# Gate projections of the first block: two matmuls a step instead of three, halves added on VectorE

## The chip, the cores and the metric

The kernel runs on one core of one Trainium2 chip. The metric is the device time of one execution, in microseconds (us). The engines are TensorE (PE, with its weight loads as PEld), VectorE (DVE), ScalarE (ACT), GpSimd (POOL) and SyncE (SP), which issues the weight DMAs.

## The reference, cut to what matters

The program is two transformer blocks on 256 tokens of width 1024, in float32. The first one is hybrid attention: a windowed grouped-query attention (16 heads, "swa") and a differential attention (8 heads, "diff"), each followed by a branch projection, and merged with sigmoid gates. The gates are what is changed here.

```python
proj = u @ w_in[l]                      # u: rms-normed tokens, w_in: 1024 x 6656
qa, ka, va, qb, kb, vb, g = jnp.split(proj, SPLITS, axis=-1)   # g: the last 2048 columns
...
gates = jax.nn.sigmoid(g + b_gate[l])
g_swa, g_diff = gates[..., :D_MODEL], gates[..., D_MODEL:]
merged = g_swa * (o_swa @ w_branch_swa[l]) + g_diff * (o_diff @ w_branch_diff[l])
```

After it come an output projection, a feed-forward block, and the whole second block (delta rule, sparse attention, cross-attention, feed-forward), which the change does not touch.

## The kernel before, in words

**Products.** Float32 products are made of three products of the shorter type fp32r. Each weight unit of 1024 x 256 (or as many elements in another shape) is loaded into `raw`. ScalarE rounds it to `whi` (high part), VectorE subtracts to get `wlo` (low part), both in two halves of 128 output features: `split(i, k)`. The activations `R1` are kept as high and low parts too, for 256 tokens side by side in one buffer (`R1b`). `feat` (lines 823 to 825) makes a half of a unit: for each of 8 slices of the contraction, high weights by high rows, high weights by low rows, low weights by high rows, each a matmul of 256 columns, all into the same 256 columns of a PSUM bank. That is 24 matmuls with 24 weight loads.

`wide` (lines 847, 848) is the form that the feed-forward blocks use: high weights by high and low rows in one matmul of 512 columns, into the two halves of a PSUM bank, then low weights by high rows into the first half. That is 16 matmuls. VectorE adds the two halves of the bank (`summed`, line 1617, a TENSOR_REDUCE).

**Gates.** There are 8 gate units of 256 features (u = 0 to 7), each of two halves j of 128. `gate` on TensorE goes through `pair`, which claims one of the three banks of the pool "gemm" for both halves and calls `feat`. On ScalarE `gate` waits for the second half and then makes two activations, tanh(0.5 x + 0.5 b), from the bank into `GA`. Later VectorE multiplies the branch projections by (1 + `GA`), in `bsw` and `bdf`.

**Order.** `schedule` writes one list of steps, by hand, and each engine goes through this list and does its own part of each step, in that order. Between the engines there are semaphores only. The units of weights stand in the order ka0, va, qa1, gate 0, qa2, gate 1, qa3, gate 2, qb0, vb0, kb0, gate 3, qb1, vb1, kb1, gate 4, qb2, vb2, kb2, gate 5, qb3, vb3, kb3, gate 6, four branch units, gate 7. The heads are woven in between: each head has stages at fixed distances (`STAGES`, `STARTS`), such as scores (L968), maxima (`s0`, `s1`: L1370 or L1519 on VectorE), exponentials (ScalarE), scaling (`n`: L1367), transposes of the probabilities (`p0`, `p1`: L809), copies of these (PT 0 by ScalarE, PT 1 by VectorE at L1504, the part for the meta tokens at L1506 or L1538), the product with V (L998 and L1003, or L1041 and L1044 for diff heads) and the output. Splits are put into the list some two units ahead of the half that uses them; a split waits until the half that used the same buffer is done.

So for the step of a gate half each engine's queue holds, around the second half of gate unit 0, for example: `split(6,0)`, scaling of head 0, gate half 1, scores and first maxima of head 1, `split(6,1)`, second maxima, exponentials, a rope unit of qa, and the two probability copies of head 0.

ScalarE's helper for activations is line 1986, VectorE's helpers are lines 1364 (scalar_tensor_tensor), 1367 (tensor_scalar) and 1370 (tensor_tensor_reduce); transposes are line 809 and the low split is line 1374. In the rows a tile name tells more than the line: `whi` is the high split, `SE<-ps,st` the tanh of a gate, `SC`, `SD` or `SE<-ps 32x256` a rope copy, `SC<-ps 128x512` the copy of PT 0.

**Banks.** The eight PSUM banks are split into "gemm" (three) and "head" (five). `claim` takes the bank whose last reader stands earliest in the list, and makes TensorE wait for that reader.

Of the kernel before, what the change touches and what calls it, by code (L numbers as in the profile page):

```python
# [10 lines left out]
ACT = mybir.ActivationFunctionType  # L11
AX = mybir.AxisListType.X
MUL, ADD, SUB, MAX = ALU.mult, ALU.add, ALU.subtract, ALU.max
# [495 lines left out]
def program(nc, A, out):  # L509
    with ExitStack() as ctx:  # L510
# [12 lines left out]
        R1 = (R1b[:, 0], R1b[:, 1], R1b)  # L523
# [16 lines left out]
        def signal(name, by=1):  # L540
            signals.append(Signal(ctx.enter_context(nc.semaphore(name)), now, by))
            return signals[-1]
# [7 lines left out]
        hi_split, lo_split = signal("hi_split"), signal("lo_split")  # L550
        gemm = signal("gemm")
# [1 line left out]
        norm_pe, norm_act, norm_dve, norm_pool = [signal("norm_" + n) for n in ("pe", "act", "dve", "pool")]  # L553
        rope_act, rope_dve, rope_pool = [signal("rope_" + n) for n in ("act", "dve", "pool")]
        val_pe, val_act, val_dve = [signal("val_" + n) for n in ("pe", "act", "dve")]
        swap_act, gate_act = signal("swap_act"), signal("gate_act")
        head_pe, head_act, head_dve, head_pool = [signal("head_" + n) for n in ("pe", "act", "dve", "pool")]
        merge_act, merge_dve, merge_pool = [signal("merge_" + n) for n in ("act", "dve", "pool")]
        post_act, post_dve, post_pool = [signal("post_" + n) for n in ("act", "dve", "pool")]
# [16 lines left out]
        def ps(*key):  # L576
            return held[key]
# [4 lines left out]
        def stat(key, n):  # L582
            if key not in stats:
                stats[key] = st[:, room[0]:room[0] + n]
                room[0] += n
                assert room[0] <= 512
            return stats[key]

        ident = ca[:, 0:128]
        half = stat("half", 16)  # L590

        def caf(name):
            return ca[:, CA[name][0]:CA[name][0] + CA[name][1]]
# [55 lines left out]
        GA = SE[:, 0:4096].rearrange("p (b n) -> p b n", b=16)  # L649
# [44 lines left out]
        rsb = {s: caf("band")[:, 256 * i:256 * i + 256] for i, s in enumerate(("nf1", "nf2"))}  # L694
# [12 lines left out]
        def normed(s):  # L707
            return lambda kt, t=1: (norm_dve, (s, "lo", kt))
# [86 lines left out]
        def tensor(e, counting):  # L795
            p = Lane(e, counting)

            def claim(pool, key, *freed):

                b = next_bank(pools[pool])  # L800
                for signal_, k in b.freed:
                    p.wait_ge(signal_, k)
                b.freed = freed
                held[key] = b.t
                return b.t
# [10 lines left out]
            def feat(o, i, j, R, n, ready, *keys):  # L816

                hi, lo = unit(i)
                c = slice(j * 128, j * 128 + 128)
                p.wait_ge(lo_split, (i, j))  # L820
                for kt in range(8):
                    p.wait_ge(*ready(kt))
                    e.matmul(o, hi[:, kt, c], R[0][:, kt, 0:n], start=kt == 0, stop=False)  # L823
                    e.matmul(o, hi[:, kt, c], R[1][:, kt, 0:n], start=False, stop=False)  # L824
                    m = e.matmul(o, lo[:, kt, c], R[0][:, kt, 0:n], start=False, stop=kt == 7)  # L825
                m.then_inc(gemm(("half", i, j), ("unit", i), *keys))

            def featk(B, i, part, R, ready, key):

                hi, lo = unit(i)  # L830
                p.wait_ge(lo_split, (i, part))
                for kt in range(4 * part, 4 * part + 4):
                    p.wait_ge(*ready(kt))
                    for j in range(2):
                        o, c = B[:, 256 * j:256 * j + 256], slice(j * 128, j * 128 + 128)
                        e.matmul(o, hi[:, kt, c], R[0][:, kt, 0:256], start=(kt, j) == (0, 0), stop=False)  # L836
                        e.matmul(o, hi[:, kt, c], R[1][:, kt, 0:256], start=False, stop=False)  # L837
                        m = e.matmul(o, lo[:, kt, c], R[0][:, kt, 0:256], start=False, stop=(kt, j) == (7, 1))  # L838
                m.then_inc(gemm(("half", i, part), ("unit", i), key))
# [210 lines left out]
            def pair(kind, u, j, i, pool, R, ready, *freed):  # L1050
                if j == 0:
                    claim(pool, (kind, u), *freed)
                if order[i][1] == "featk":
                    return featk(ps(kind, u), i, j, R, ready, (kind, u))
                feat(ps(kind, u)[:, 256 * j:256 * j + 256], i, j, R, 256, ready, (kind, u))

            def gate(u, j, i):
                pair("gate", u, j, i, "gemm", R1, normed("n1"), (gate_act, u))

            def bsw(u, j, i):  # L1060
                pair("bsw", u, j, i, "gemm", R3a, lambda kt: (head_dve, ("ol", nth["swa", kt])), (merge_dve, ("bs", u)))
# [262 lines left out]
            def cross(h, part):  # L1324
# [17 lines left out]
                if part == "o":  # L1342
                    B = claim("four", ("xo", h), (cross_dve, ("ox", h)))
                    p.wait_ge(cross_dve, ("pt", h))
                    for j in range(2):
# [3 lines left out]
                    m.then_inc(cross_pe(("xo", h)))  # L1349

            parts = {"turn": turn, "turnx": turnx, "rsb": rsb_, "rope": rope, "ropek": ropek, "turnm": turnm, "v": v, "vt": vt, "swa": swa, "diff": diff, "gate": gate, "bsw": bsw, "bdf": bdf,
                     "out": out_, "mem": mem, "upg": upg, "upu": upu, "down": down, "tail": tail, "conv": conv, "zg": zg,
                     "delta": delta, "dsa": dsa, "dsah": dsah, "xq": xq, "cross": cross}
# [6 lines left out]
        def vector(e, counting):  # L1360
            d = Lane(e, counting)
# [237 lines left out]
            def chunk(u):  # L1599
# [8 lines left out]
                for t in range(2):  # L1608
                    d.wait_ge(post_dve, ("p1", t, u))
                    e.tensor_tensor(X[:, t, c], X[:, t, c], junk["p1"][:, 1024 + 1024 * t:2048 + 1024 * t][:, c], ADD).then_inc(post_dve(("p1", "x", u, t)))  # L1610

            def summed(kind, f, j, b):

                B = ps(kind, f, j, b)
                at = 256 * b + (512 if kind == "u" else 0)
                d.wait_ge(gemm, (kind, f, j, b))
                e.tensor_reduce(FSLOT[j % 2][0][:, at:at + 256], B[:, :].rearrange("p (a n) -> p n a", a=2), AX, ADD).then_inc(  # L1617
                    ffn_dve((kind, f, j, b)))
# [12 lines left out]
            def upg(f, j, part, i):  # L1631
                if j in WIDE:
                    summed("g", f, j, part)
                if part and j:
                    scaled_gate(f, j)
# [297 lines left out]
            def final():  # L1933
# [33 lines left out]
                for hf in range(2):  # L1967
# [4 lines left out]

            e.memset(half, -0.5).then_inc(set_dve("half"))
            e.memset(ones, 1.0).then_inc(set_dve("one"))
            parts = {"split": split, "rows": rows, "turn": turn, "turnx": turnx, "stat": stat_, "rsb": rsb_, "chunk": chunk, "chunk2": chunk2, "upg": upg, "setup": setup, "rotate": rotate, "turnm": turnm, "vt": vt, "swa": swa, "diff": diff,
                     "bsw": bsw, "bdf": bdf, "post": post, "upu": upu, "zc": zc, "tail": tail, "taps": taps, "zg": zg,
                     "delta": delta, "dsa": dsa, "dsah": dsah, "add": add, "squares": squares, "cross": cross, "final": final}
            for now[0], (name, *a) in enumerate(plan):
# [3 lines left out]
        def scalar(e, counting):  # L1982
            a = Lane(e, counting)

            def act(o, i, f=ACT.Copy, **kw):
                return e.activation(o, i, f, **kw)  # L1986
# [124 lines left out]
            def gate(u, j, i):  # L2111
                if j:
                    a.wait_ge(pc_in, 0)
                    a.wait_ge(gemm, ("gate", u))
                    a.wait_ge(set_dve, "hb")
                    for k in range(2):
                        act(GA[:, 2 * u + k, :], ps("gate", u)[:, 256 * k:256 * k + 256], ACT.Tanh,
                            bias=hb[:, 2 * u + k:2 * u + k + 1], scale=0.5).then_inc(gate_act(u))

            def merge(u):  # L2120
# [227 lines left out]
            def final():  # L2348
# [6 lines left out]
                for hf in range(2):  # L2355
# [10 lines left out]
            e.dma_start(pc[:, 0:8], A["params"][:, 0:8]).then_inc(mix_in(0), 16)  # L2366
            parts = {"split": split, "rows": rows, "turn": turn, "turnx": turnx, "stat": stat_, "setup": setup, "rope": rope, "roped": roped, "turnm": turnm, "swap": swap, "v": v, "swa": swa,
                     "diff": diff, "gate": gate, "merge": merge, "mem": mem, "psq": psq, "post": post, "upg": upg, "upu": upu, "conv": conv,
                     "convs": convs, "zg": zg, "delta": delta, "dsa": dsa, "dsah": dsah, "squares": squares, "xq": xq, "cross": cross,
                     "final": final}  # L2370
# [189 lines left out]
        for _ in range(2):  # L2560
            for engine in (tensor, vector, scalar, gpsimd, sync):
                engine(Count(), True)
            rewind()
# [6 lines left out]
        @block.vector  # L2570
        def _(e):
            vector(e, False)
# [57 lines left out]
```

## Time and profile before

| | us |
|---|---|
| median of 3 runs | 960.5 (960.37 to 960.55) |
| the profiled execution | 960.5 |
| its span | 958.4 |
| TensorE busy | 937.5 (98%), 6180 matmuls |
| VectorE busy | 674.6 (70%) |
| ScalarE busy | 527.3 (55%) |
| GpSimd busy | 137.9 (14%) |

The span runs from the first to the last instruction; what is over in the execution's time lies around it. Matmuls are pipelined, and the ends of their rows are modelled, so their rows overlap: what a matmul costs is read from where the next one starts. The granted clock of TensorE is 0.999 over the span, that is 2.4 GHz throughout. A line of the timeline has the start (us from the span's start), the duration, the engine, line, operation, tiles, shapes, how many instructions are merged in it, and in brackets the idle time of the engine before it with what ended it.

### The profile page before, as it was taken

The numbers are of one execution on the slowest core, as the hardware profiler recorded it, in microseconds if no ns is written. First come the engines' busy times: TensorE is split into PE (matmuls) and PEld (weight loads), VectorE is DVE, ScalarE is ACT, GpSimd is POOL, SyncE is SP. The second block draws the span as 40 slices with busy tenths as digits, with TensorE's granted clock in tenths as the row PEclk, the third lists the DMA queues.
The fourth block names the chain that finished last, engine by engine and source line by source line (L and its number), as shares of the span: only waits on it lengthen the run. The fifth ranks groups of instructions, "written<-read, shape, count | busy, mean of one in ns | idle before, by whom it ended". The sixth has DMA issues, their size and how long they took to land.

```text
span 958.4 us, 15483 instructions
## 1 busy us (share of the span) xinstructions
PE 937.5 (98%) x6180; PEld 840.1 (88%) x6180; DVE 674.6 (70%) x1233; ACT 527.3 (55%) x1013; POOL 137.9 (14%) x159
## 2 busy tenths in 40 slices
PE   8999999999999999999999999899999999999996
PEld 7989888999999988888898899888798898888885
DVE  6888777777478676776758668767665567666765
ACT  6876665875456644444446686455454454344443
POOL 2211111220133000000001119941100000000001
PEclk9999999999999999999999999999999999999999
DMA  9544324343367555555565563300543455656441
GB/s 316 183 155 132 128 93 136 129 133 133 133 229 243 169 204 194 176 194 198 176 216 185 177 237 123 121 30 1 176 149 117 153 176 176 220 176 205 166 156 45
DMA packets 115863, 154.71 MB, mean 161 GB/s; under 512 B 2728, under 2 KB 98224, under 8 KB 115536
## 3 DMA queue, kind: packets, MB, share of 16 engines
q1 hardware_dynamic: 113376, 142.91, 44.9%
q0 software_dynamic: 1952, 10.42, 3.0%
q8 instruction: 49, 0.80, 0.4%
q10 hardware_dynamic: 464, 0.40, 0.2%
q14 instruction: 22, 0.18, 0.1%
HBM read 150.56 MB, written 3.16 MB: 160 GB/s over the span
## 4 chain that ended last, share of the span: by engine, by line
PE 89%; DVE 3%; POOL 3%; ACT 3%; issue 1%; DMA 0%; POOLq 0%; DVEq 0%; ACTq 0%
PE ps L847 14%; PE ps L823 8%; PE ps L825 8%; PE ps L824 8%; PE ps L848 7%; PE ps L1135 4%; PE ps L1108 4%; PE ps L1109 4%; PE ps L1110 4%; PE ps L866 4%; PE ps L868 4%; PE ps L867 4%; PE ps L809 3%; PE ps L836 2%; PE ps L838 2%; PE ps L837 2%
## 5 line engine op out<-in xcount | busy, mean ns | idle before, releaser
L1374 DVE TENSOR_TENSOR wlo<-raw,whi 128x1024 fp32r<-128x1024 f32 (+1 forms) x268 | 327.7, 1242 | 164.4 <-ACT whi L1986 164.0
L1986 ACT ACTIVATE whi<-raw 128x1024 fp32r<-128x1024 f32 (+1 forms) x268 | 273.8, 1050 | 129.9 <-PE ps L848 53.5
L847 PE MATMUL ps<-R1b,whi 128*128 128x512 f32 x576 | 201.8, 393 | 0.0
L823 PE MATMUL ps<-R1b,whi 128*128 128x256 f32 (+1 forms) x592 | 172.3, 291 | 0.8 <-DVE wlo L1374 0.8
L825 PE MATMUL ps<-R1b,wlo 128*128 128x256 f32 (+1 forms) x592 | 167.7, 283 | 0.0
L824 PE MATMUL ps<-R1b,whi 128*128 128x256 f32 (+1 forms) x592 | 167.5, 283 | 0.0
L848 PE MATMUL ps<-R1b,wlo 128*128 128x256 f32 x576 | 161.4, 280 | 0.0
L847 PEld LDWEIGHTS ps<-R1b,whi 128*128 128x128 f32 x576 | 108.1, 188 | 24.7 <-issue 0.5
L823 PEld LDWEIGHTS ps<-R1b,whi 128*128 128x128 f32 x592 | 111.6, 188 | 9.1 <-issue 7.9
L825 PEld LDWEIGHTS ps<-R1b,wlo 128*128 128x128 f32 x592 | 111.8, 189 | 0.0
L824 PEld LDWEIGHTS ps<-R1b,whi 128*128 128x128 f32 x592 | 111.5, 188 | 0.2
L848 PEld LDWEIGHTS ps<-R1b,wlo 128*128 128x128 f32 x576 | 108.2, 188 | 0.6
L2380 POOL TENSOR_TENSOR st<-st 128x1 f32<-128x1 f32 (+5 forms) x28 | 23.3, 838 | 375.4 <-DVE st L1367 299.8
L1108 PE MATMUL ps<-whi,R3ah 128*128 128x512 f32 x176 | 68.8, 391 | 0.0
L1109 PE MATMUL ps<-wlo,R3ah 128*128 128x512 f32 x176 | 68.8, 391 | 0.0
L1110 PE MATMUL ps<-whi,R3al 128*128 128x512 f32 x176 | 68.5, 389 | 0.0
L1986 ACT ACTIVATE F<-F 128x512 f32<-128x512 f32 (+6 forms) x58 | 28.9, 502 | 59.7 <-DVE F L1628 53.7
L1986 ACT ACTIVATE R3ah<-F 128x512 fp32r<-128x512 f32 x22 | 13.9, 632 | 68.1 <-DVE F L1650 68.1
L1617 DVE TENSOR_REDUCE F<-ps 128x256 f32<-128x512 f32 x72 | 49.3, 684 | 0.0
L1986 ACT ACTIVATE SC<-ps 128x512 f32<-128x512 f32 (+3 forms) x78 | 33.1, 429 | 21.0 <-PE ps L825 10.3
L1108 PEld LDWEIGHTS ps<-whi,R3ah 128*128 128x128 f32 x176 | 33.0, 188 | 7.2
L1110 PEld LDWEIGHTS ps<-whi,R3al 128*128 128x128 f32 x176 | 33.0, 188 | 7.2
(293 smaller groups left out, 1780.2 us busy)
## 6 DMA issues: line engine op xcount, KB each, us to landing
raw<-in_w_in SPq DMA_DIRECT2D x34, 1024.0 KB, 5.1
raw<-in_w_ffn_in SPq DMA_DIRECT2D x22, 1024.0 KB, 5.1
raw<-in_w_ffn_out SPq DMA_DIRECT2D x11, 1024.0 KB, 5.4
raw<-in_w_gate SPq DMA_DIRECT2D x11, 1024.0 KB, 5.3
raw<-in_w_up SPq DMA_DIRECT2D x11, 1024.0 KB, 5.3
raw<-in_w_down SPq DMA_DIRECT2D x11, 1024.0 KB, 6.0
raw<-in_w_out SPq DMA_DIRECT2D x8, 1024.0 KB, 5.1
raw<-in_w_xkv SPq DMA_DIRECT2D x8, 1024.0 KB, 5.5
```

The costliest lines, as they stand in the source:

```text
L823: e.matmul(o, hi[:, kt, c], R[0][:, kt, 0:n], start=kt == 0, stop=False)
L824: e.matmul(o, hi[:, kt, c], R[1][:, kt, 0:n], start=False, stop=False)
L825: m = e.matmul(o, lo[:, kt, c], R[0][:, kt, 0:n], start=False, stop=kt == 7)
L847: e.matmul(B[:, :].rearrange("p (a n) -> p a n", a=2), hi[:, kt, c], R[2][:, :, kt, 0:256], start=kt == 0, stop=False)
L848: m = e.matmul(B[:, 0:256], lo[:, kt, c], R[0][:, kt, 0:256], start=False, stop=kt == 7)
L866: e.matmul(B[:, 0:n], R[0][:, kt, c], hi[:, k, :], start=kt == 0, stop=False)
L1108: e.matmul(B[:, :], Fh[:, k, c], hi[:, k, d], start=j == 0 and k == 0, stop=False)
L1109: e.matmul(B[:, :], Fh[:, k, c], lo[:, k, d], start=False, stop=False)
L1110: m = e.matmul(B[:, :], Fl[:, k, c], hi[:, k, d], start=False, stop=end and k == 1)
L1374: e.tensor_tensor(half_of(wlo[i % HL], i, k), half_of(raw[i % RAW], i, k), f32(half_of(whi[i % HL], i, k)), SUB).then_inc(lo_split(i, (i, k)))
L1617: e.tensor_reduce(FSLOT[j % 2][0][:, at:at + 256], B[:, :].rearrange("p (a n) -> p n a", a=2), AX, ADD).then_inc(ffn_dve((kind, f, j, b)))
L1986: return e.activation(o, i, f, **kw)
```

## The change

TensorE's `gate` claims a bank of its own for each half and calls `wide`: 8 steps of one 512-column and one 256-column matmul. VectorE gets a step `gate`, at the same place of the list: it waits for that half's matmuls and adds the two halves of the bank into `GA`. ScalarE's two tanhs stay at the place of the second half, each waits for VectorE's addition of its half, and they read `GA` and write it in place. The schedule, the splits, the DMAs and everything else stay.

```diff
-        swap_act, gate_act = signal("swap_act"), signal("gate_act")
+        swap_act, gate_act, gate_dve = signal("swap_act"), signal("gate_act"), signal("gate_dve")
...
             def gate(u, j, i):
-                pair("gate", u, j, i, "gemm", R1, normed("n1"), (gate_act, u))
+                B = claim("gemm", ("gate", u, j), (gate_dve, (u, j)))
+                p.wait_ge(lo_split, (i, j))
+                wide(B, i, j, R1, normed("n1")).then_inc(gemm(("half", i, j), ("unit", i), ("gate", u, j)))
...
+            def gate(u, j, i):
+                d.wait_ge(gemm, ("gate", u, j))
+                e.tensor_reduce(GA[:, 2 * u + j, :], ps("gate", u, j)[:, :].rearrange("p (a n) -> p n a", a=2), AX, ADD).then_inc(
+                    gate_dve((u, j)))
...
             def gate(u, j, i):
                 if j:
                     a.wait_ge(pc_in, 0)
-                    a.wait_ge(gemm, ("gate", u))
                     a.wait_ge(set_dve, "hb")
                     for k in range(2):
-                        act(GA[:, 2 * u + k, :], ps("gate", u)[:, 256 * k:256 * k + 256], ACT.Tanh,
+                        a.wait_ge(gate_dve, (u, k))
+                        act(GA[:, 2 * u + k, :], GA[:, 2 * u + k, :], ACT.Tanh,
                             bias=hb[:, 2 * u + k:2 * u + k + 1], scale=0.5).then_inc(gate_act(u))
```

## Rows read from the trace of the kernel before

**Rows 1.** The page, part 1: busy us, share of the span, instructions.
```profile
PE 937.5 (98%) x6180; PEld 840.1 (88%) x6180; DVE 674.6 (70%) x1233; ACT 527.3 (55%) x1013; POOL 137.9 (14%) x159
```

**Rows 2.** Windows, the stretch of gate units 0 to 2 (stretch, length, busy us and count).
```profile
39.69:90.95 51.26, 51.26 (x418) 47.10 (x417) 43.48 (x123) 39.87 (x97) 10.68 (x12) 1.00 0.42 138
```

**Rows 3.** Timeline, TensorE, first matmuls of two successive halves made by `feat`.
```profile
109.79 0.28 PE L823 MATMUL ps<-R1b,whi 128*128 128x256 f32 x1
...
112.63 0.28 PE L823 MATMUL ps<-R1b,whi 128*128 128x256 f32 x1
```

**Rows 4.** Timeline, TensorE, first matmuls of two successive halves made by `wide`.
```profile
329.55 0.39 PE L847 MATMUL ps<-R1b,whi 128*128 128x512 f32 x1
...
332.34 0.39 PE L847 MATMUL ps<-R1b,whi 128*128 128x512 f32 x1
```

**Rows 5.** The page, part 5: busy us, mean ns of one, idle before.
```profile
L824 PEld LDWEIGHTS ps<-R1b,whi 128*128 128x128 f32 x592 | 111.5, 188 | 0.2
...
L1617 DVE TENSOR_REDUCE F<-ps 128x256 f32<-128x512 f32 x72 | 49.3, 684 | 0.0
```

**Rows 6.** Timeline, VectorE, around gate unit 0.
```profile
45.86 1.22 DVE L1374 TENSOR_TENSOR wlo<-raw,whi 128x1024 fp32r<-128x1024 f32 x1 [0.83 <-ACT whi L1986]
...
48.50 0.49 DVE L1370 CUSTOM_DVE_ANT_0 SC<-ps,ca,pc 128x272 f32<-128x272 f32 x1
...
49.74 1.22 DVE L1374 TENSOR_TENSOR wlo<-raw,whi 128x1024 fp32r<-128x1024 f32 x1
...
52.72 0.28 DVE L1506 COPY SC<-ps 128x128 f32<-128x128 f32 x1
```

**Rows 7.** Timeline, ScalarE, around gate unit 0.
```profile
45.86 0.84 ACT L1986 ACTIVATE SE<-ps,st 128x256 f32<-128x256 f32 x2
46.59 1.06 ACT L1986 ACTIVATE whi<-raw 128x1024 fp32r<-128x1024 f32 x1
...
52.41 0.60 ACT L1986 ACTIVATE SC<-ps 128x512 f32<-128x512 f32 x1
```

**Rows 8.** Timeline, TensorE, the first matmuls with V of heads 0, 1 and 2.
```profile
53.35 0.61 PE L998 MATMUL ps<-SC,SD 128*128 128x128 f32 x4
...
65.82 0.60 PE L998 MATMUL ps<-SC,SD 128*128 128x128 f32 x4
...
78.29 0.61 PE L998 MATMUL ps<-SC,SD 128*128 128x128 f32 x4
```

**Rows 9.** Timeline, VectorE, around gate units 1 and 2.
```profile
64.70 0.68 DVE L1504 COPY SC<-ps 128x512 f32<-128x512 f32 x1
65.30 0.28 DVE L1506 COPY SC<-ps 128x128 f32<-128x128 f32 x1
...
77.56 0.28 DVE L1506 COPY SC<-ps 128x128 f32<-128x128 f32 x1
...
80.31 1.23 DVE L1374 TENSOR_TENSOR wlo<-raw,whi 128x1024 fp32r<-128x1024 f32 x1 [1.34 <-ACT whi L1986]
```

**Rows 10.** Timeline, ScalarE, behind the tanhs of gate unit 1.
```profile
63.99 0.59 ACT L1986 ACTIVATE SC<-ps 128x512 f32<-128x512 f32 x1
```

**Rows 11.** Timeline, around gate unit 3: VectorE, ScalarE, TensorE.
```profile
112.69 1.18 DVE L1367 TENSOR_SCALAR SC<-SC,st 128x272 f32<-128x272 f32 x4
...
115.67 1.58 ACT L1986 ACTIVATE SD<-ps 32x256 f32<-32x256 f32 x4 [1.05 <-PE ps L825]
...
117.92 0.73 PE L968 MATMUL ps<-F 64*128 64x272 f32 x4 [0.65 <-ACT SC L1986]
```

**Rows 12.** Timeline, around gate unit 7: ScalarE, VectorE, TensorE.
```profile
254.69 0.60 ACT L1986 ACTIVATE SC<-ps 128x512 f32<-128x512 f32 x1
...
255.25 0.40 DVE L1538 COPY F<-ps 16x256 f32<-16x256 f32 x1
...
256.50 0.72 PE L1041 MATMUL ps<-F,SC 128*128 128x128 f32 x5
```

More of the change, by code:

```diff
@@ L1974, in vector @@
             e.memset(ones, 1.0).then_inc(set_dve("one"))
-            parts = {"split": split, "rows": rows, "turn": turn, "turnx": turnx, "stat": stat_, "rsb": rsb_, "chunk": chunk, "chunk2": chunk2, "upg": upg, "setup": setup, "rotate": rotate, "turnm": turnm, "vt": vt, "swa": swa, "diff": diff,
+            parts = {"split": split, "rows": rows, "gate": gate, "turn": turn, "turnx": turnx, "stat": stat_, "rsb": rsb_, "chunk": chunk, "chunk2": chunk2, "upg": upg, "setup": setup, "rotate": rotate, "turnm": turnm, "vt": vt, "swa": swa, "diff": diff,
                      "bsw": bsw, "bdf": bdf, "post": post, "upu": upu, "zc": zc, "tail": tail, "taps": taps, "zg": zg,
```

## The prediction

> **What bounds the kernel now.** I read the page's busy shares first: TensorE is busy 98% of the span [rows 1]. A busy matmul row is longer than its slot, so I then read the engine timeline for where one half of a weight unit starts and where the next does: 24 matmuls of 256 columns take 112.63 - 109.79 = 2.84 us [rows 3], although each row is 0.28 us long. The windows view of the stretch from the first gate unit to the end of the third, 39.69 to 90.95, comes next [rows 2]: TensorE has no gap there, VectorE works 43.5 of 51.3 us (85%) and ScalarE 39.9 (78%). So TensorE sets the end, and the two others have little room just where the first three gate units stand. The last view is the timeline of the three engines side by side around each gate half. It shows how far VectorE and ScalarE run behind TensorE, and which of their results TensorE takes almost at the moment it is ready. The stage of attention that multiplies by V begins at 53.35, 65.82 and 78.29 [rows 8]. The last copy it needs from VectorE (the key tokens of the meta part, L1506) ends at 52.72 + 0.28 = 53.00, at 65.30 + 0.28 = 65.58 and at 77.56 + 0.28 = 77.84 [rows 6, 9]. The room is 0.35, 0.24 and 0.45 us. These are the places where something late becomes a gap of TensorE.
>
> **Part 1: the matmuls.** A half loses eight weight loads and eight matmuls, and its columns stay the same (three times 256 against 512 + 256). The feed-forward blocks already run this form: a half takes 332.34 - 329.55 = 2.79 us [rows 4] against 2.84. The removed loads read 188 ns each [rows 5], yet the slot of a 256-column matmul with its load is 2.84 / 24 = 0.118 us, so the loads run beside the streaming and only some 6 ns per step are to be had: 0.05 us a half, 0.74 us over the 16 halves if nothing else moved (2.840 and 2.793 before rounding the starts; from the two-digit rows it is 0.05 x 16 = 0.8).
>
> The Trainium skill, page TensorE: Matmul & The Clock Gate, section Back-to-back issue gap, gives a sustained 131 ns for 512 columns behind a load. By that figure the wide form would save about 0.1 us in each of 128 steps, 13 us; the starts of rows 4 contradict it, since 16 matmuls in 2.79 us leave about 0.23 us for the wide one.
>
> **Part 2: the additions on VectorE.** 16 reductions 128x512 to 128x256 from PSUM, 684 ns each by the same form in the feed-forward blocks [rows 5]. Consecutive rows of VectorE overlap by 0.08 us (a copy of 0.68 us at 64.70 is followed by the next at 65.30 [rows 9]), so one costs 0.60 us of its queue. That is 9.6 us of work, which is free only where VectorE would have waited.
>
> **Part 3: the tanh behind the addition.** The two tanhs of a unit took 0.84 us together right at the end of the matmuls [rows 7]. The second now waits for VectorE to arrive at its addition. Behind it on ScalarE stand the high split of a coming weight half, the exponentials, the rope copies and the copy of P (transposed probabilities) that V needs; behind the split stands VectorE's low split. From SBUF in place I take the tanh at the same 0.42 us; the bounds are 0.3 and 0.5 and move the sum by under 0.3 us.
>
> **First gate unit.** The addition of half 0 falls in the 0.83 us for which VectorE waits ahead of its split at 45.86 [rows 6]: free. That of half 1 comes after the scaling of the head's probabilities, ahead of the row at 48.50, and ends at 48.50 + 0.68 = 49.18. The second tanh then ends about 49.65. ScalarE's high split moves from 46.59 to 49.6 and ends at 50.66 [rows 7], where before it was done long ahead of its use. The low split at 49.74 [rows 6] becomes 50.7: VectorE is 0.95 late, of which 0.60 is the addition and the rest the wait. The meta copy ends at 53.95, and the P copy, which was at 52.41 for 0.60, ends at 53.9. TensorE starts V at 54.0 instead of 53.35: 0.65 us lost.
>
> **Second gate unit.** Both queues come in 0.9 late. The addition of half 0 makes VectorE 1.5 late; that of half 1 goes ahead of the copy at 64.70, so it runs 66.2 to 66.9. Second tanh to 67.3. The P copy stands directly behind the tanhs on ScalarE (63.99 for 0.59 [rows 10]) and moves to 67.3 to 67.9: 3.3 late. The meta copy ends at 65.58 + 0.9 + 1.2 = 67.7. TensorE starts V at 67.75 instead of 65.82; the total is 1.9 us.
>
> **Third gate unit.** ScalarE carries its 3.3 us on, and VectorE takes it over by the low split that waits for ScalarE's high split. TensorE is only 1.9 late, so the queues have lost 1.4 on it. One addition (half 0) more, and the meta copy ends at 77.84 + 3.3 + 0.6 = 81.75. V starts at 81.8 instead of 78.29: total 3.5 us. The addition of half 1 comes with a tanh wait too, but ahead of the next split at 80.31 VectorE had 1.34 us of waiting [rows 9], and the three weight units behind it hold no additions: I take it that the queues catch up with TensorE there and that no further time is lost.
>
> **Later units.** At units 3 and 4 TensorE already waits 0.65 us for the P copy, as in the row at 117.92 [rows 11]. That copy stands behind four rope copies, before which ScalarE had 1.05 us of idle time (115.67). The scaling ends at 112.69 + 1.18 = 113.87; addition to 114.55, tanh to 115.05, high split (1.06) to 116.05, so the rope copies begin 0.35 to 0.4 later. 0.35 and 0.3 us. Units 5 and 6 have room: nothing. At unit 7 VectorE's addition of half 1 stands behind the low split, ahead of the row at 255.25 [rows 12], and ends at 255.93; tanh to 256.4, P copy to 257.0 instead of 254.69 + 0.60 = 255.29. TensorE starts this head's V at 256.50, so 0.45 us. The shorter matmuls count in units 3 to 7 only, ten halves: -0.46. Ahead of a V stage that waits for the other engines they give nothing.
>
> **Banks.** A gate unit took one of three PSUM banks for both halves; now each half takes one. By the order of claims, each then waits for the reader of the half three before it, two halves (5.7 us) back or more, and even 3.3 us of delay leaves that covered. I put it at 0; should a cosine product on VectorE be late once, it is 0.5.
>
> **The sum.** 3.5 + 0.35 + 0.3 + 0.45 - 0.46 = +4.1 us. The profiled execution took 960.5 us (span 958.4 and 2.1 around it), the same as the median before, so the forecast is 964.6 us.
>
> **Rivals.**
> (a) The slips are taken up: each V stage has more room than the ends of the copies tell, or the order of additions and tanhs leaves the queues level by the next unit. Then only the matmuls count, and at most half of the delay: 959.8 to 962.2. For it: VectorE still has 15% of idle time in [rows 2] and the 1.34 us wait. Against it: rooms of 0.24 to 0.45 us at three successive V stages, and 0.6 us per addition.
> (b) Faster, by the loads: if a weight load is not beside the streaming but ahead of it, a step saves up to 0.188 us, 128 steps 24 us, and even at a tenth of that in place of the 6 ns the time would be about 958. It decides from the point where a load saved is worth more than 0.04 us a step, enough to outweigh the 4.6 us of waits. Against it: starts 0.118 us apart with 188 ns loads, and the wide half at 2.79.
> (c) Slower still: the 3.3 us slip of ScalarE does not shrink in the stretch after unit 2, and every one of the 16 additions (9.6 us) shows in TensorE: 970. It needs VectorE to be the bound throughout; from 95 us on it has more idle time between waits (1.05 and 0.65 us at each rope), so I doubt it.
>
> **Chances.** Forecast 0.80, (a) 0.12, (b) 0.02, (c) 0.06. The likeliest gives 964.6. The range 961.5 to 968.0 leaves out most of (a), (b) and (c), 0.2. A measurement of this kernel can tell 0.2%, 1.9 us, from no change: slower is above 962.4, which the forecast passes and (c) too, less a bit of the forecast's low end, 0.84; within it 0.12; faster, below 958.6, 0.04.
>
> **What would show it.** In the profile after, a gate half should take about 2.79 us (2.84 would fail part 1). The reductions should be 16 rows of 0.68 us. A gap of TensorE ahead of the V stages (L998, L1003) near 53, 66 and 79 us should appear, released by a VectorE copy or by ScalarE, of about 0.65, 1.3 and 1.6 us; the second tanh of each unit should stand right behind an addition; the row at 46.59 should stand near 49.6. No such gaps and a time near 960 would make the forecast wrong, and so would gaps that wait for a bank or for a low split.

## The result

| | before | after |
|---|---|---|
| median | 960.52 us (6 runs, 960.37 to 962.24) | 965.04 us (6 runs, 964.76 to 965.15) |
| ratio | | 1.0042, 95% interval 1.0029 to 1.0055 |
| profiled execution, its span (us) | 960.5, 958.4 | 965.15, 963.0 |

The forecast was 964.6 in a range of 961.5 to 968.0, so the change is slower by nearly what was said: 4.5 us measured, 4.1 forecast. The trace shows that this agreement holds two misses of opposite sign: TensorE loses 1.4 us more than forecast, and the last store gives 1.0 back.

The page, part 1, of the kernel after, beside [rows 1] (128 matmuls fewer, 16 VectorE instructions more):

```profile
PE 939.3 (98%) x6052; PEld 834.6 (87%) x6052; DVE 684.3 (71%) x1249; ACT 527.6 (55%) x1013; POOL 137.6 (14%) x159
```

The lines view has the additions and, by form and over the first 270 us, the tanhs. Columns: count, busy us, mean ns of one, idle time before them. The first row is from the source view of L1616 (minimum, median and maximum ns, first and last start).

```profile
L1616 DVE TENSOR_REDUCE SE<-ps x16: 675/684/689, 45.1 to 260.2; 128x256 f32<-128x512 f32 x16
...
L1993 ACT ACTIVATE SE<-SE,st 128x256 f32<-128x256 f32 x16 | 8.0, 503 | 17.4 <-DVE SE L1616 17.4
```

The tanhs (ScalarE's helper is now line 1993) sit behind 17.4 us of idle time that ends with VectorE's addition. In the kernel before, this group read:

```profile
L1986 ACT ACTIVATE SE<-ps,st 128x256 f32<-128x256 f32 x16 | 6.7, 468 | 5.7 <-PE ps L825 5.7
```

The windows view of the stretch that answers to [rows 2], from the first gate unit to the fourth V stage (columns: stretch, length, busy us and count of TensorE, its weight loads, VectorE, ScalarE and GpSimd, granted clock, DMA share, GB/s):

```profile
39.69:94.70 55.01, 51.98 (x371) 44.88 (x370) 47.24 (x129) 40.01 (x97) 10.47 (x12) 1.00 0.39 129
```

It is 55.01 us long and was 51.26 with TensorE busy throughout. Now TensorE has 55.01 - 51.98 = 3.03 us of gaps, and VectorE 3.76 us more work. The timeline of TensorE names the gaps (0.62 + 0.99 + 1.42 = 3.03) and the later ones; [rows 8, 11, 12] hold the same matmuls of before:

```profile
54.15 0.71 PE L998 MATMUL ps<-SC,SD 128*128 128x128 f32 x4 [0.62 <-DVE SC L1508]
...
67.86 0.71 PE L998 MATMUL ps<-SC,SD 128*128 128x128 f32 x4 [0.99 <-DVE SC L1508]
...
81.94 0.60 PE L998 MATMUL ps<-SC,SD 128*128 128x128 f32 x3 [1.42 <-DVE SC L1508]
...
121.95 0.73 PE L968 MATMUL ps<-F 64*128 64x272 f32 x4 [1.01 <-ACT SC L1993]
...
184.40 0.82 PE L809 MATMUL ps<-ca,SC 128*16 128x128 f32 x6 [0.21 <-ACT SC L1993]
...
197.20 0.82 PE L809 MATMUL ps<-ca,SC 128*16 128x128 f32 x6 [0.41 <-ACT SC L1993]
...
261.99 0.71 PE L1041 MATMUL ps<-F,SC 128*128 128x128 f32 x4 [0.35 <-ACT SC L1993]
```

L1508 is the copy of the meta part that was L1506. A bracket counts from the modelled end of the matmul before, which overlaps the next slot by some 0.15 us, so a loss is a little more than its bracket. The loss is therefore taken from the starts of the same matmuls in two traces. I call it the shift. Here it is for eight kernels, always minus the kernel before, in us (the column is the start in the kernel before). The runs e4 and e8 are the programs of e9 and e10; e1, e2 and e7 are told in their places:

| first matmul with V at | 53.3 | 65.8 | 78.3 | 105.3 | 121.5 | 155.1 | 183.5 | 196.3 | 245.7 | 256.5 |
|---|---|---|---|---|---|---|---|---|---|---|
| gate unit passed | 0 | 1 | 2 | | 3 | 4 | 5 | 5 | 6 | 7 |
| after | 0.80 | 2.04 | 3.64 | 3.75 | 4.01 | 4.26 | 4.57 | 5.16 | 5.05 | 5.49 |
| e3_tanh_late | 0.28 | 1.58 | 1.59 | 1.58 | 1.46 | 1.37 | 1.67 | 1.67 | 1.56 | 1.49 |
| e9_both_late_again | -0.04 | -0.13 | -0.11 | -0.11 | -0.21 | -0.31 | -0.38 | -0.38 | -0.49 | -0.57 |
| e5_units_012 | 0.51 | 1.73 | 3.34 | 3.44 | 3.41 | 3.41 | 3.41 | 3.42 | 3.41 | 3.41 |
| e6_units_3to7 | 0.05 | 0.05 | 0.05 | 0.05 | 0.29 | 0.54 | 0.86 | 1.43 | 1.32 | 1.75 |
| e10_not_5_again | 0.80 | 2.04 | 3.63 | 3.74 | 4.00 | 4.26 | 4.26 | 4.26 | 4.15 | 8.25 |
| e11_spare_bank | 0.68 | 1.90 | 3.49 | 3.61 | 3.85 | 4.10 | 4.12 | 4.11 | 4.01 | 4.44 |
| e12_banks_swapped | 0.78 | 2.00 | 3.61 | 3.71 | 3.95 | 4.22 | 4.53 | 5.11 | 5.00 | 9.09 |

Traces differ by up to 0.2 us already before the first gate unit. In the kernel after, the shift stays at about 5.6 us to the issue of the last output store, but the span grows by 4.6 only. The missing 1.0 us is in the last store, which lands 0.9 us faster, and in rounding. DMA view of the last stretch, first of the kernel before (953 to 958), then of the kernel after (945 to 963); columns of a store are count, KB, us from issue to landing:

```profile
q14 instruction: 1, 0.01, 0.4%
...
out<-F ACTq DMA_DIRECT2D x1, 256.0 KB, 3.5
```

```profile
q14 instruction: 1, 0.01, 0.1%
...
out<-F ACTq DMA_DIRECT2D x1, 256.0 KB, 2.6
```

In the kernel before, a packet of the instruction queue q14 starts at about 956.5 us, among the packets of that store, and the store lands after 3.5 us. In the kernel after it comes at 946.7, ahead of all stores, and the store lands after 2.6.

### The profile page after: what moved, and what is told of

Same layout as the page of the kernel before. It is cut to its first block, busy times and chain, and to the rows that moved or that the text cites. A ratio compares the mean times of both kernels' runs of the same rounds, so it can differ in the third digit from the quotient of the medians.

```text
span 963.0 us, 15251 instructions
## 1 busy us (share of the span) xinstructions
PE 939.3 (98%) x6052; PEld 834.6 (87%) x6052; DVE 684.3 (71%) x1249; ACT 527.6 (55%) x1013; POOL 137.6 (14%) x159
## 4 chain that ended last, share of the span: by engine, by line
PE 78%; ACT 8%; DVE 8%; POOL 3%; issue 2%; DMA 0%; POOLq 0%; DVEq 0%; ACTq 0%
PE ps L847 15%; PE ps L848 8%; PE ps L823 5%; PE ps L825 5%; PE ps L824 5%; PE ps L1137 4%; PE ps L1110 4%; PE ps L1111 4%; PE ps L1112 4%; PE ps L866 4%; PE ps L868 4%; PE ps L867 4%; ACT whi L1993 3%; PE ps L809 2%; DVE wlo L1376 2%; ACT SC L1993 2%
## 5 line engine op out<-in xcount | busy, mean ns | idle before, releaser
L847 PE MATMUL ps<-R1b,whi 128*128 128x512 f32 x704 | 248.0, 394 | 0.0
L848 PE MATMUL ps<-R1b,wlo 128*128 128x256 f32 x704 | 197.3, 280 | 0.0
L847 PEld LDWEIGHTS ps<-R1b,whi 128*128 128x128 f32 x704 | 132.2, 188 | 31.9 <-issue 2.7
L823 PE MATMUL ps<-R1b,whi 128*128 128x256 f32 (+1 forms) x464 | 135.3, 292 | 0.8 <-DVE wlo L1376 0.8
L825 PE MATMUL ps<-R1b,wlo 128*128 128x256 f32 (+1 forms) x464 | 131.7, 284 | 0.0
L824 PE MATMUL ps<-R1b,whi 128*128 128x256 f32 (+1 forms) x464 | 131.6, 284 | 0.0
L823 PEld LDWEIGHTS ps<-R1b,whi 128*128 128x128 f32 x464 | 87.4, 188 | 6.9 <-issue 6.4
L824 PEld LDWEIGHTS ps<-R1b,whi 128*128 128x128 f32 x464 | 87.4, 188 | 0.2
```

Source lines behind the costliest of these rows:

```text
L847: e.matmul(B[:, :].rearrange("p (a n) -> p a n", a=2), hi[:, kt, c], R[2][:, :, kt, 0:256], start=kt == 0, stop=False)
L848: m = e.matmul(B[:, 0:256], lo[:, kt, c], R[0][:, kt, 0:256], start=False, stop=kt == 7)
```

## The experiments

All were timed against the kernel before on the same chip, and the ratios are to it. The edits are shown against the kernel after, except that of e7, which is made to the kernel before. e1 to e4, e11 and e12 ran on one chip, e5 to e8 on another; e9 and e10 repeat two programs on a third.

**e1_banks**: a bank for each half, and nothing else of the change.

```diff
-                B = claim("gemm", ("gate", u, j), (gate_dve, (u, j)))
-                p.wait_ge(lo_split, (i, j))
-                wide(B, i, j, R1, normed("n1")).then_inc(gemm(("half", i, j), ("unit", i), ("gate", u, j)))
+                B = claim("gemm", ("gate", u, j), (gate_act, (u, j)))
+                feat(B[:, 0:256], i, j, R1, 256, normed("n1"), ("gate", u, j))
...
-            def gate(u, j, i):
-                d.wait_ge(gemm, ("gate", u, j))
-                e.tensor_reduce(GA[:, 2 * u + j, :], ...)
...
-                        act(GA[:, 2 * u + k, :], GA[:, 2 * u + k, :], ACT.Tanh,
+                        act(GA[:, 2 * u + k, :], ps("gate", u, k)[:, 0:256], ACT.Tanh,
```

> Only the banks of the change: each gate half claims a bank of its own, but is made of 24 narrow matmuls as before, and the two tanhs read the banks directly (no addition on VectorE). My theory (the loss comes from the additions and the tanh that waits for them) expects the time of before, 960.5 us within 0.3, and no gap of TensorE ahead of the V stages. The rival that the shorter life of banks makes TensorE wait expects up to +4.6.

Measured: 961.79, ratio 1.0016 (1.0007 to 1.0025). The expectation, 960.5 within 0.3, missed this by 1.3. The V stages of units 0 to 2 have no gap, as expected, but the rival, that banks make TensorE wait, is right at one place. No stage moves by more than 0.02 us until gate unit 7; there TensorE loses 1.2 us at once. The first bdf unit always takes bank 0, and half (7,0) now holds it until ScalarE's tanh, which stands behind a high split. Timelines of TensorE and ScalarE of e1:

```profile
254.49 0.39 PE L836 MATMUL ps<-R3bh,whi 128*128 128x256 f32 x1 [0.91 <-ACT SE L1987]
```

```profile
253.02 1.06 ACT L1987 ACTIVATE whi<-raw 128x1024 fp32r<-128x1024 f32 x1 [4.36 <-PE ps L825]
253.98 0.82 ACT L1987 ACTIVATE SE<-ps,st 128x256 f32<-128x256 f32 x2
```

In the kernel after, VectorE's addition frees this bank early, at 255.41 + 0.68 = 256.09, and there is no such wait. Banks cost nothing there, but only by who frees them and by which half lies in bank 0; e12 returns to this.

**e2_no_add**: wide matmuls, no addition; the tanh reads the first half of the bank, so the product of high weights and low rows is missing from the gates.

```diff
-                B = claim("gemm", ("gate", u, j), (gate_dve, (u, j)))
+                B = claim("gemm", ("gate", u, j), (gate_act, (u, j)))
...
-            def gate(u, j, i):
-                d.wait_ge(gemm, ("gate", u, j))
-                e.tensor_reduce(GA[:, 2 * u + j, :], ...)
...
-                        act(GA[:, 2 * u + k, :], GA[:, 2 * u + k, :], ACT.Tanh,
+                        act(GA[:, 2 * u + k, :], ps("gate", u, k)[:, 0:256], ACT.Tanh,
```

> The wide matmuls and a bank a half, but no addition: the tanh reads the first half of the bank from PSUM, and the product of high weights by low rows, which is in the second half, is left out of the gates. My theory expects 959.8 us (16 halves at 2.79 instead of 2.84 us: -0.74), since nothing waits. The rival that a weight load saved is worth its 188 ns expects far less, up to 24 us; the rival that the wide form itself slows something expects 960.5 or more.

Measured: 960.98, ratio 1.0005 (0.9996 to 1.0015). TensorE gains 0.37 us over the first 14 halves, then loses 1.09 at unit 7 by the same bank wait as in e1. The expectation missed that wait and so came out 1.2 too low.

**e3_tanh_late**: additions in place, the tanhs of seven units later in ScalarE's order, where nothing urgent waits behind them.

```diff
+TANH_AFTER = {('swa', 0, 't'): 0, ('swa', 1, 't'): 1, ('swa', 2, 't'): 2, ('swa', 6, 'x0'): 3, ('diff', 0, 'x0'): 4, ('split', 23, 0): 5, ('diff', 7, 'v'): 7}
...
-                if j:
+                if j and (i is None or u not in TANH_AFTER.values()):
...
+                if (name, *a_) in TANH_AFTER:
+                    gate(TANH_AFTER[(name, *a_)], 1)
```

> The kernel after, with ScalarE's tanhs of all units but 6 moved back in its queue to places where it was idle; VectorE's additions stay where they are. This takes the tanh's wait from in front of the high split and the copy of P. By hand from the rows of before: V of head 0 is 0.3 late instead of 0.65, of head 1 1.6 late instead of 1.9, of head 2 nothing more; units 3, 4 and 7 lose nothing; the ten halves left give -0.46. So 961.6 us, some 3 us less than after. If the additions alone are the loss, it stays at 965.0; if the tanh's wait alone is, it comes to 959.8.

Measured: 960.99, ratio 1.0004 (0.9995 to 1.0014), 0.6 under the expectation, which left out the faster last store and put 0.3 too little on TensorE. Of the 5.5 us at unit 7 only 1.5 are left: the tanhs' waits for VectorE cost 4.0 us, the additions 1.5 + 0.6 (what the matmuls save) = 2.1. Two gaps remain ahead of V; the starts behind them are 0.3 and 1.3 us later, half an addition's queue time and two, by what VectorE adds before the copy. A third of 0.21 us stands at unit 5, ahead of the transposes. Timeline of TensorE of e3:

```profile
53.62 0.71 PE L1000 MATMUL ps<-SC,SD 128*128 128x128 f32 x4 [0.26 <-DVE SC L1510]
67.40 0.71 PE L1000 MATMUL ps<-SC,SD 128*128 128x128 f32 x4 [0.99 <-DVE SC L1510]
```

**e4_both_late** and, the same program again, **e9_both_late_again**: nine of the 16 additions are moved later in VectorE's order as well, behind the copies that TensorE waits for.

```diff
+SUM_AFTER = {('rotate', 'qa', 4, 6): [(0, 1)], ('swa', 1, 'p1'): [(1, 0)], ('split', 8, 1): [(1, 1)], ('split', 10, 0): [(2, 0)], ('split', 14, 1): [(3, 1)], ('split', 18, 1): [(4, 1)], ('diff', 1, 'p'): [(5, 0)], ('split', 22, 1): [(5, 1)], ('diff', 7, 'p'): [(7, 1)]}
```

> As e3, and the additions too are moved back in VectorE's queue to places behind the copies that V needs, where it was idle, at most two halves later, so that the bank comes free in time. My theory expects that all the waits go and the shorter matmuls stay: 959.8 us, faster than before by 0.7. The rival that VectorE's 9.6 us of additional work costs time wherever it stands expects 962 or more.

> The kernel after with both orders changed (the additions of nine halves later in VectorE's order, the tanhs of seven units later in ScalarE's), the same program as in the earlier run of it, on more rounds. Theory of the order: 959.0, 0.9985 of the kernel before, from 0.6 us of shorter matmuls and 0.96 us of a shorter last store. Rival, the earlier gain was scatter between executions: 960.5, ratio 1.000 with an interval that holds 1.

Measured: 958.94, ratio 0.9985 (0.9976 to 0.9994), and again 958.93, ratio 0.9983 (0.9974 to 0.9991). The expectation of 959.8 lacked only the last store. This version is faster than the kernel before by 0.2% and than the kernel after by 0.6%. Windows and timeline of e9:

```profile
39.69:90.95 51.26, 51.26 (x371) 44.87 (x371) 46.70 (x129) 39.90 (x97) 11.71 (x12) 1.00 0.42 138
```

```profile
53.31 0.61 PE L1002 MATMUL ps<-SC,SD 128*128 128x128 f32 x4
```

TensorE is busy throughout again, although VectorE does 46.70 - 43.48 = 3.2 us more work than in [rows 2]. The additions and tanhs are all still there: their places cost time, their number does not. Of the 1.6 us gained, 0.6 is the shorter matmuls and 1.0 the last store (e7).

**e5_units_012**: the change in units 0 to 2 only. **e6_units_3to7**: in the others only.

```diff
+WIDE_GATES = (0, 1, 2)
...
+                if u not in WIDE_GATES:
+                    return pair("gate", u, j, i, "gemm", R1, normed("n1"), (gate_act, u))
```

> The change in gate units 0, 1 and 2 alone, units 3 to 7 as before. My theory expects TensorE to be 3.7 us late behind unit 2 (in the profile after it was 3.75 at the V stage of head 3) and the same 3.7 us at the last output stores; with the last store as slow as before (3.5 us) the time is 964.2, with the fast one (2.6 us) 963.3. A rival in which each unit costs the same expects 3/8 of 5.6 us, 962.6.

> The change in gate units 3 to 7 alone. If the delays of the two groups are independent, TensorE ends 5.57 - 3.75 = 1.8 us late: 962.3 us with the slow last store, 961.4 with the fast one. If the later delays only come because the queues are still late from unit 2, it is 960.0 (the shorter matmuls of ten halves alone).

Measured: e5 965.42, ratio 1.0051 (1.0035 to 1.0066), its four executions at 964.1 to 967.5; e6 961.45, ratio 1.0004 (0.9995 to 1.0014), as expected for independent delays and the fast last store. The shifts add up: 3.41 + 1.75 = 5.16 against 5.49, of which 0.1 to 0.3 is the difference at the first V stage. The time of e5 is not the expected 963.3, though its last store is fast (2.6 us). Its shift of 3.4 us stays until 500 us, and in the profiled execution it grows to 7.3 us around one gap in the second block, which is longer than in the kernel before and is followed by a stretch at half the granted clock (0.5, 1.2 GHz). TensorE's timelines of the kernel before and of e5:

```profile
609.67 0.47 PE L866 MATMUL ps<-whi,R1b 128*128 128x512 f32 x1 [1.58 <-ACT F L1986]
```

```profile
614.43 0.77 PE L868 MATMUL ps<-whi,R1b 128*128 128x512 f32 x1 [3.30 <-ACT F L1999]
```

Windows of e5 (the last three columns are granted clock, DMA share, GB/s):

```profile
613.20:616.60 3.40, 2.17 (x5) 1.82 (x6) 2.84 (x6) 3.36 (x7) 3.18 (x3) 0.50 0.00 0
616.60:620.00 3.40, 3.40 (x9) 2.63 (x9) 3.30 (x11) 0.01 (x1) 3.08 (x4) 0.50 0.00 0
```

The clock falls at 613.21, still inside the gap, so the gap is not its consequence; ScalarE waits there for GpSimd until 611.89, in the kernel before until 607.13, which is more than the shift; why stays open. The one execution of e5 with a mean clock of 0.999 took 964.1, still 1.0 above 960.56 + 3.4 - 0.9 = 963.1. That execution has no profile, and what made the 1.0 stays open.

**e7_pad**: the kernel before with 16 tiny memsets on VectorE in a feed-forward stage, the gates untouched.

```diff
+                if f == "f1" and part == 0 and j in (2, 3, 4, 5):
+                    for k in range(4):
+                        e.memset(stat("pad", 16)[:, 4 * j + k - 8:4 * j + k - 7], 0.0).then_inc(set_dve("pad"))
```

> The kernel before with 16 tiny memsets (128x1) added to VectorE's program in the first feed-forward block, where VectorE is idle for much of the time; gates untouched. In the profiles after, e3 and e4 the last output store takes 2.6 us to land, in those of before, e1 and e2 3.5 us, and there an 8 KB instruction packet of queue 14 lies among its packets. Theory: the packet belongs to VectorE's (or ScalarE's) code, and 16 more instructions move it ahead of the store: 959.5 us, the last store at 2.6 us. Rival: the tail has another cause, and the time stays at 960.5.

Measured: 959.55, ratio 0.9989 (0.9979 to 0.9999), as expected, with the last store at 2.6 us and the q14 packet at 941.0 in place of 956.5. Sixteen more instructions on VectorE make the kernel 1.0 us faster without touching the gates. In all kernels here with additions (6 to 16 of them) or with the memsets the store lands in 2.6 us, in the kernel before, e1 and e2 in 3.5. The packet goes by the number of VectorE's instructions: less TensorE's shift, it stands at 956.5 with none more, at 953.0 with 6 (e5), at 950.1 with 10 (e6) and at 941.2 with 14 or 16. It lies among the last store's packets in those three kernels only. That the packet itself holds up the store is inferred from this; no run moved it alone.

**e8_not_5** and, the same program again, **e10_not_5_again**: unit 5 as before.

```diff
+WIDE_GATES = (0, 1, 2, 3, 4, 6, 7)
```

> The kernel after with gate unit 5 as before. I had put unit 5 at 0; in the profile after TensorE comes out of units 5 and its two followers 0.9 us later. If unit 5's additions and tanh wait are the cause, the two new gaps near 184 and 197 us go and the time is 965.0 - 0.9 = 964.1. If the cause is the lateness brought along from units 3 and 4, it stays at 965.0.

> The kernel after with gate unit 5 as before, the same program as in the earlier run of it, whose executions all held stretches of TensorE at half the granted clock. Theory (unit 5 costs 0.9 us in the kernel after): 964.1 in an execution without such a stretch. Rival, the mixed form costs time of itself: 967 to 969 again in each execution, at a granted clock of 0.998.

Measured: 969.04 (1.0086, 1.0071 to 1.0101) and 968.16 (1.0080, 1.0067 to 1.0094). The theory of unit 5 missed the time in both, and the rival of e8 too. The rival of e10, that the mixed form costs time of itself, named this time but not the clock (0.995 to 0.997 against 0.998); e11 decides on it. The shift says that unit 5 did cost 0.9 (4.26 against 5.16 at 196.3), and then 4.1 us come at unit 7. By the order of claims in the program, the form with one bank for unit 5 claims one bank fewer, so every later claim takes another bank, and half (7,1) comes to lie in bank 0.

**e11_spare_bank**: e10 with one more claim, of a bank that nothing writes, which restores the turn of the banks. **e12_banks_swapped**: the kernel after with the banks of the two halves of unit 7 swapped.

```diff
                 if u not in WIDE_GATES:
+                    if j:
+                        claim("gemm", ("spare", u), (gate_act, u))
                     return pair("gate", u, j, i, "gemm", R1, normed("n1"), (gate_act, u))
```

```diff
-                B = claim("gemm", ("gate", u, j), (gate_dve, (u, j)))
+                B = claim(f"bank{1 - j}" if u == 7 else "gemm", ("gate", u, j), (gate_dve, (u, j)))
```

> The kernel after with gate unit 5 as before, and one more bank claimed and left unused in that unit, so that the turn of the three banks is again that of the kernel after: gate half (7,1) no longer stands in bank 0, which the first bdf unit claims two matmul groups later. Theory (the extra 4 us of the form without the spare bank are that wait, 2.4 us, and the 3.4 us stretch at half clock behind it, 1.7): no gap at 258 us, no half clock there, 964.1, shift of TensorE 4.3 at 245 us. Rival (the mixed form itself, or a stretch at half clock that comes by itself): 967 to 969 as before.

> The kernel after with one edit: the two halves of gate unit 7 take banks 1 and 0 in place of 0 and 1, so that the first bdf unit, which claims bank 0, waits for the addition of half (7,1). Theory: a gap of about 2.3 us ahead of that unit near 259 us, released by VectorE's addition, which takes in the 0.35 us wait at 262, and a stretch at half clock behind it worth 1.7: 965.0 + 1.9 + 1.7 = 968.7; without the half clock 967.0. Rival (bank order is worth nothing): 965.0.

Measured: e11 964.40, ratio 1.0039 (1.0027 to 1.0052); e12 968.91, ratio 1.0080 (1.0067 to 1.0094). Both are what the bank theory said, within 0.3 us, and both rivals fall. One claim that moves no data is worth 968.16 - 964.40 = 3.8 us. TensorE's loss at unit 7 in e12 is 9.09 - 5.00 = 4.09 us: 2.4 of it the wait for the bank and 1.7 a stretch at half the granted clock. In the kernel after 0.44 is lost there anyway, so the wait alone is worth 2.0. TensorE, VectorE and windows of e12:

```profile
260.92 0.39 PE L836 MATMUL ps<-R3bh,whi 128*128 128x256 f32 x1 [2.41 <-DVE SE L1616]
```

```profile
259.03 1.22 DVE L1376 TENSOR_TENSOR wlo<-raw,whi 128x1024 fp32r<-128x1024 f32 x1 [2.48 <-ACT whi L1993]
260.18 0.68 DVE L1616 TENSOR_REDUCE SE<-ps 128x256 f32<-128x512 f32 x1
```

```profile
258.50:260.90 2.40, 0.00 (x1) 0.00 (x0) 1.86 (x3) 0.91 (x3) 0.00 (x0) 1.00 0.00 0
...
262.00:263.00 1.00, 1.00 (x7) 1.00 (x7) 0.00 (x0) 0.00 (x0) 0.00 (x0) 0.50 0.00 0
263.00:264.00 1.00, 1.00 (x6) 1.00 (x6) 0.00 (x0) 0.00 (x0) 0.00 (x0) 0.50 0.08 16
```

The bdf unit waits for the addition of half (7,1), which stands behind a low split that waits for ScalarE. Behind the gap of 2.4 us the clock granted is half for 3.4 us, from 261.47 on. The execution of e12 with a mean clock of 0.999 took 967.17, 2.1 above the kernel after; the other four took 968.6 to 970.2. In the kernel after bank 0 holds half (7,0), whose addition is long done, and the only gap at this place is the one at 261.99.

## Why the prediction was right, and where it was not

**Part 1, the matmuls: right.** A half in the kernel after starts at 113.50 and the next unit at 116.30, so it takes 2.80 (2.79 forecast), on the timeline of TensorE:

```profile
113.50 0.40 PE L847 MATMUL ps<-R1b,whi 128*128 128x512 f32 x1
...
116.30 0.28 PE L823 MATMUL ps<-R1b,whi 128*128 128x256 f32 x1
```

In e9, where no wait hides it, the shift goes from -0.11 to -0.57 over units 3 to 7: -0.46, the forecast term. The removed loads gave back what the starts had said, and rival (b) is excluded. Its price of about 958 also left out the 4.6 us of waits that its next sentence names: a tenth of 0.188 us in 128 steps is 2.4 us, and 960.5 + 4.6 - 2.4 is 962.7.

The Trainium skill (TensorE: Matmul & The Clock Gate, Back-to-back issue gap) gives a sustained 131 ns for a matmul of 512 columns with its load. The trace does not agree: here a step of 2.80 / 8 = 0.35 us, less 0.118 for its 256-column matmul, leaves 0.23 us.

**Units 0 to 2: right, 3.75 against 3.5.** Forecast were cumulative losses of 0.65, 1.9 and 3.5, measured 0.80, 2.04 and 3.64, with 0.16 of that there before the first gate unit. The steps are in the timelines of ScalarE (first fence) and VectorE (second) of the kernel after:

```profile
45.85 0.50 ACT L1993 ACTIVATE SE<-SE,st 128x256 f32<-128x256 f32 x1
49.33 0.51 ACT L1993 ACTIVATE SE<-SE,st 128x256 f32<-128x256 f32 x1 [2.98 <-DVE SE L1616]
49.75 1.04 ACT L1993 ACTIVATE whi<-raw 128x1024 fp32r<-128x1024 f32 x1
...
53.43 0.60 ACT L1993 ACTIVATE SC<-ps 128x512 f32<-128x512 f32 x1
...
67.04 0.51 ACT L1993 ACTIVATE SE<-SE,st 128x256 f32<-128x256 f32 x1 [1.65 <-DVE SE L1616]
67.46 0.58 ACT L1993 ACTIVATE SC<-ps 128x512 f32<-128x512 f32 x1
...
83.65 0.51 ACT L1993 ACTIVATE SE<-SE,st 128x256 f32<-128x256 f32 x1 [1.71 <-DVE SE L1616]
```

```profile
48.61 0.68 DVE L1616 TENSOR_REDUCE SE<-ps 128x256 f32<-128x512 f32 x1
...
50.83 1.23 DVE L1376 TENSOR_TENSOR wlo<-raw,whi 128x1024 fp32r<-128x1024 f32 x1 [0.28 <-ACT whi L1993]
...
53.81 0.28 DVE L1508 COPY SC<-ps 128x128 f32<-128x128 f32 x1
...
66.32 0.68 DVE L1616 TENSOR_REDUCE SE<-ps 128x256 f32<-128x512 f32 x1
66.92 0.68 DVE L1506 COPY SC<-ps 128x512 f32<-128x512 f32 x1
67.52 0.28 DVE L1508 COPY SC<-ps 128x128 f32<-128x128 f32 x1
69.01 1.23 DVE L1376 TENSOR_TENSOR wlo<-raw,whi 128x1024 fp32r<-128x1024 f32 x1 [1.21 <-ACT whi L1993]
...
72.80 1.57 DVE L1376 TENSOR_TENSOR wlo<-raw,whi 128x1024 fp32r<-128x1024 f32 x1 [0.33 <-ACT whi L1993]
...
80.40 0.68 DVE L1616 TENSOR_REDUCE SE<-ps 128x256 f32<-128x512 f32 x1
...
81.60 0.28 DVE L1508 COPY SC<-ps 128x128 f32<-128x128 f32 x1
```

ScalarE is idle for 2.98 us, then does the second tanh at 49.33; the high split of [rows 7] moved from 46.59 to 49.75 (forecast 49.6), the low split of [rows 6] to 50.83 (50.7), the meta copy to 53.81 + 0.28 = 54.09 (53.95). At the second unit both the addition at 66.32 and the wait of 1.65 us stand ahead of the copies. At the third, VectorE waits for ScalarE's late high splits (1.21 and 0.33 us) and does one addition ahead of the copy that ends at 81.88 (forecast 81.75). e3 splits these 3.6 us into 1.6 by the additions and 2.0 by the tanhs. Behind unit 2 nothing more is lost (3.75 at 91.0 and at 105.3), as the idle 1.34 us of [rows 9] had suggested; so rival (a) and rival (c) both fall.

**Units 3, 4 and 7: right.** 4.01 - 3.66 = 0.35 (forecast 0.35), 4.26 - 3.93 = 0.33 (0.3), and 5.49 - 5.05 = 0.44 (0.45); 3.66 and 3.93 are the shifts just ahead of those waits, at L968 of 116.5 and 150.1. The wait at 121.95 is 1.01, where [rows 11] had 0.65.

**Unit 5: wrong, put at nothing, cost 0.9.** The step that failed is "Units 5 and 6 have room: nothing". I had looked at the copy ahead of V, which does have room there. What was late is the exponentials of a later head. The bank that the transposes of probabilities (L809) write is the one from which these exponentials read the scores, so TensorE waits for them. Timeline of ScalarE and of TensorE of the kernel before (not shown above), then ScalarE of the kernel after:

```profile
178.41 0.49 ACT L1986 ACTIVATE SC<-ps,st 128x272 f32<-128x272 f32 x1 [1.42 <-DVE st L1367]
...
190.61 0.49 ACT L1986 ACTIVATE SC<-ps,st 128x272 f32<-128x272 f32 x1
```

```profile
179.82 0.81 PE L809 MATMUL ps<-ca,SC 128*16 128x128 f32 x6
...
192.06 0.82 PE L809 MATMUL ps<-ca,SC 128*16 128x128 f32 x6
```

```profile
183.26 0.49 ACT L1993 ACTIVATE SC<-ps,st 128x272 f32<-128x272 f32 x1 [2.01 <-DVE st L1369]
...
196.10 0.49 ACT L1993 ACTIVATE SC<-ps,st 128x272 f32<-128x272 f32 x1 [0.59 <-DVE st L1369]
```

Against a TensorE that is 4.27 late the exponentials are 183.26 - 178.41 - 4.27 = 0.58 late, one addition of VectorE ahead of the maxima that they need; against 4.57 the second pair is 196.10 - 190.61 - 4.57 = 0.92 late, because the tanh at 186.39 waited 1.70 us and the splits behind it passed that on. The room at both places was some 0.4 us: the exponentials with their accumulator reads (two, 0.20 us after the last one's 0.48) end at 179.45 and 191.66, and TensorE came at 179.82 and 192.06. So 0.2 and 0.5 of gap follow, shown as 0.21 at 184.40 and 0.41 at 197.20. Both are waits for a bank, which the prediction had named as a sign of being wrong; they did mark a term that it had wrong. e6, e10 and e11 confirm the size: with unit 5 changed the shift rises by 0.9 there, without it by nothing.

**The shorter matmuls: -0.3 in the kernel after.** They count between the waits only; units 5 and 7 give nothing of theirs, since those wait.

**Banks: 0 was right for this kernel, but the bounds were wrong.** The prediction allowed 0.5 us by way of a late cosine product. e8, e10 and e12 show what one other turn of the same three banks costs: 2.0 us by the wait, and 3.6 in the starts behind it with the half clock that followed. The claim of bank 0 by name, by the bdf unit, was the thing to look at.

**The end: not foreseen.** A shift of 5.6 us becomes 4.6 in the span, by the last store. So 4.1 was forecast; it was 5.6 (0.9 more for unit 5, 0.25 more in units 0 to 2, 0.2 less given back by the matmuls, some 0.1 spread over the rest) less 1.0. That the total came within 0.5 us was partly luck: without the last store's gain it would have been 966.0. The mechanism and its places, other than unit 5, were not luck.

## What to carry to other kernels

An engine whose queue is written in a fixed order pays for a new dependency by what stands behind it, not by the work added: here 16 additions of 0.68 us and 16 waits cost 5.6 us at the places where they were put, and nothing once they stood behind the copies that TensorE needs. List for every late stage of the two helping engines each thing that TensorE takes from them, the release of a bank as well as the operand. When a step claims more banks, write down which half lies in a bank that a later step takes by name.

## What the runs showed of the hardware

- The last 256 KB store lands in 3.5 us in the three kernels where an instruction packet of 8 KB falls among its packets, and in 2.6 in the eleven where it does not. The packet moves with the number of VectorE's instructions, so two kernels can differ by 1.0 us (0.1%) for a reason that has nothing to do with their edit (e7).
- TensorE was granted half its clock (0.5) for single stretches in the middle of some executions: of 3.4 us at unit 7 in the profiles of e8, e10 and e12, starting 0.3 to 1.1 us behind the gap of 2.4 us, and of 6.8 us in that of e5. In the profiles of e2, e6, e8 and e12 another of 3.4 us starts 2.0 to 2.5 us behind a gap of 1.2 us near 680 us and makes TensorE 1.5 to 1.6 us later; the ten other profiles have the same gap and no stretch. The gaps of up to 1.42 us at the V stages had none. All nine executions of e8 and e10 have a mean clock of 0.995 to 0.997 and took 967.85 us or more, but one of the five of e12, the same in program, had 0.999 and took 967.17. Why a stretch comes in one execution and not in the next stays open.
- After the last matmul every profile ends at half the granted clock (in the kernel before from 956.1 us on, the last matmul ends at 950.8), and that end lowers the mean too: the profile of e1 has 0.997 without any other stretch, that of e10 has 0.997 with one. The mean alone tells a stretch among the matmuls only where it is below that.
- A tanh from SBUF in place took 503 ns, from PSUM 468 ns, at the same 128x256.
